# One engine for a whole step: who spreads the turned pages in the compression of a decoder's paged cache

## What is computed

```python
def compress_rows(a, pe, w1, w2):
    n = a.shape[0] // CMP_STRIDE
    seg = a.reshape(n, CMP_STRIDE, N_KV, HEAD_DIM)
    nxt = jnp.concatenate([seg[1:], jnp.zeros_like(seg[:1])], axis=0)
    blk = jnp.concatenate([seg, nxt], axis=1) + pe[None, :, None, :]
    flat = blk.transpose(0, 2, 1, 3).reshape(n, N_KV, CMP_LEN * HEAD_DIM)
    return jax.nn.gelu(flat @ w1) @ w2
...
    k_cmp = compress_rows(rows[:, 0], pe[0], w_c1[0], w_c2[0])
    v_cmp = compress_rows(rows[:, 1], pe[1], w_c1[1], w_c2[1])
```

## Time and profile before

| | us |
|---|---|
| median of 3 runs | 2296.28 (2295.02 to 2296.4) |
| the profiled execution | 2291.58 |
| its span in the profile | 2289.8 |
| the compression stage in it | 971.15 to 1216.00 |
| PE busy in the span | 2010.6 (88%) |
| VectorE busy | 1374.4 (60%) |
| ScalarE busy | 927.0 (40%) |

### The profile page before, as it was taken

The page is one execution under the profiler, slowest core; times in us unless marked ns, Lnnn a source line. Parts: engine busy times, 40 slices in busy tenths (PEclk is TensorE's granted clock), DMA queues, the critical chain, the costliest instruction groups (busy, mean ns, idle before and its releaser), DMA issues.

```text
span 2289.8 us, 28365 instructions
## 1 busy us (share of the span) xinstructions
PE 2010.6 (88%) x10404; PEld 1589.5 (69%) x10404; DVE 1374.4 (60%) x1788; ACT 927.0 (40%) x1229; POOL 115.7 (5%) x154
## 2 busy tenths in 40 slices
PE   5997767879999986599996878799999999999994
PEld 3655523669997454577774556688888888888883
DVE  4423685337773123377774222588888888888885
ACT  0112001100000011167762441277777777777773
POOL 0000000000001000000000000011001111111000
PEclk8997555689999976599997887799999999999997
DMA  7433003044566320034434873289999999999993
GB/s 274 147 101 80 1 6 115 1 129 154 168 176 220 129 102 0 8 122 137 148 120 139 297 293 107 88 322 358 364 351 343 346 342 346 346 354 355 369 346 116
DMA packets 194637, 453.18 MB, mean 198 GB/s; under 512 B 11719, under 2 KB 77375, under 8 KB 193250
## 3 DMA queue, kind: packets, MB, share of 16 engines
q1 hardware_dynamic: 187082, 414.64, 51.5%
q0 software_dynamic: 7456, 37.24, 5.0%
HBM read 439.04 MB, written 21.27 MB: 201 GB/s over the span
## 4 chain that ended last, share of the span: by engine, by line
PE 70%; DVE 8%; ACT 3%; issue 3%; DMA 2%; SPq 1%; POOLq 0%; DVEq 0%; POOL 0%; ACTq 0%
PE bank L2196 63%; PE bank L2199 7%; ACT arena L2692 2%; SPq L2062 1%; DMA arena<-in_cache_nsa 1%; ACT L2692 1%; DVE uT L2455 0%; DMA ring<-in_cache_nsa 0%; DMA arena<-in_w_moe_gu 0%; ACT ring L2692 0%; DVE arena L2590 0%; DMA ring<-scr_y,mkv 0%; DVE arena L794 0%; DVE rtmp L2448 0%; ACT arena_r L2692 0%
## 5 line engine op out<-in xcount | busy, mean ns | idle before, releaser
L2196 PE MATMUL bank<-arena_r 128*128 128x448 f32 (+2 forms) x3296 | 812.9, 361 | 18.3 <-DVE uT_r L648 11.3
L2196 PEld LDWEIGHTS bank<-arena_r 128*128 128x128 f32 x3296 | 607.0, 189 | 94.7 <-issue 15.4
L1680 DVE TENSOR_TENSOR ring_r<-ring,arena_r 128x1792 fp32r<-128x1792 f32 (+1 forms) x216 | 443.8, 2088 | 49.0 <-ACT arena_r L2692 47.6
L2692 ACT ACTIVATE arena_r<-ring 128x1792 fp32r<-128x1792 f32 (+1 forms) x216 | 370.2, 1727 | 136.0 <-PE bank L2196 133.2
L2196 PE MATMUL bank<-arena 128*32 128x256 f32 (+20 forms) x1498 | 284.2, 386 | 60.6 <-DVE arena L2576 25.0
L2692 ACT ACTIVATE arena<-bank 128x512 f32<-128x512 f32 (+11 forms) x312 | 138.6, 457 | 369.5 <-PE bank L2196 243.1
L2196 PEld LDWEIGHTS bank<-arena 128*128 128x128 f32 (+13 forms) x1498 | 194.9, 202 | 131.6 <-issue 69.2
L2196 PE MATMUL bank<-ring_r,arena_r 128*128 128x448 f32 (+1 forms) x840 | 246.0, 374 | 0.0
L2692 ACT ACT_TABLE_LOAD x57 | 73.1, 1283 | 425.3 <-DVE rtmp L2448 144.7
L2199 PE MATMUL bank<-consts_sb,arena 128*128 128x128 f32 (+9 forms) x788 | 143.7, 318 | 106.8 <-DVE arena L794 19.5
L2199 PEld LDWEIGHTS bank<-consts_sb,arena 128*128 128x128 f32 (+9 forms) x788 | 97.4, 160 | 162.6 <-issue 43.2
(11 more groups left out here) (341 smaller groups left out, 1904.2 us busy)
## 6 DMA issues: line engine op xcount, KB each, us to landing
ring<-in_w_moe_gu SPq DMA_DIRECT2D x144, 896.0 KB, 7.0
ring<-in_w_moe_d SPq DMA_DIRECT2D x60, 1024.0 KB, 6.6
ring<-in_cache_nsa SPq DMA_DIRECT2D x176, 256.0 KB, 4.5
arena<-in_w_moe_gu SPq DMA_DIRECT2D x48, 896.0 KB, 6.3
ring<-in_w_ffn_gu SPq DMA_DIRECT2D x22, 1024.0 KB, 7.4
arena<-in_cache_nsa SPq DMA_DIRECT2D x80, 256.0 KB, 6.1
ring<-in_w_in_a SPq DMA_DIRECT2D x8, 1536.0 KB, 7.8
arena<-in_w_moe_d SPq DMA_DIRECT2D x12, 1024.0 KB, 6.7
```

The costliest lines, as they stand in the source:

```text
L1680: V.tensor_tensor(unit_low(c), unit_slot(c), unit_high(c), ALU.subtract).then_inc(S("m_sp"), 1)
L2196: return nc.tensor.matmul(out, lhsT, rhs, start=first, stop=last, **kw_)
L2692: return nc.scalar.activation(out, in_, fn, **kw_)
```

## The change

ScalarE makes all four copies of the even steps and VectorE all four of the odd steps. PE's waits follow: a turn waits for one engine only, the one that copied the bank two steps before, and a group's product for two steps of each. VectorE's and ScalarE's other work keeps its steps; on a step that an engine doesn't copy it also no longer waits for the turn.

```diff
@@ turn(t), on PE
-                for part in range(2):
-                    pe.wait_ge(S(f"xe{part}"), 4 + t - 1)
+                if t == 0:
+                    pe.wait_ge(S("xe0"), 4)
+                    pe.wait_ge(S("xe1"), 4)
+                if t >= 2:
+                    pe.wait_ge(S(f"xe{t % 2}"), 4 + t // 2)
@@ mul(t), on PE
                 if t % 4 == 0:
                     for part in range(2):
-                        pe.wait_ge(S(f"xe{part}"), 4 + t + 4)
+                        pe.wait_ge(S(f"xe{part}"), 4 + t // 2 + 2)
@@ compress_dve
             for t in range(STEPS):
-                dve.wait_ge(S("ct"), 4 + t + 1)
-                if t % 4 == 0:
-                    dve.wait_ge(S("cm"), 2 + max(0, t - 8))
-                for r in range(2):
-                    link(V.tensor_copy(*piece(t, 1, r)), "xe1", r == 1)
+                if t % 2:
+                    dve.wait_ge(S("ct"), 4 + t + 1)
+                    if t % 4 == 1:
+                        dve.wait_ge(S("cm"), 2 + max(0, t - 9))
+                    for n in range(4):
+                        link(V.tensor_copy(*piece(t, n // 2, n % 2)), "xe1", n == 3)
@@ compress_act
             for t in range(STEPS):
-                act.wait_ge(S("ct"), 4 + t + 1)
-                if t % 4 == 0:
-                    act.wait_ge(S("cm"), 2 + max(0, t - 8))
-                for r in range(2):
-                    link(f(*piece(t, 0, r), ACT.Copy), "xe0", r == 1)
+                if t % 2 == 0:
+                    act.wait_ge(S("ct"), 4 + t + 1)
+                    if t % 4 == 0:
+                        act.wait_ge(S("cm"), 2 + max(0, t - 8))
+                    for n in range(4):
+                        link(f(*piece(t, n // 2, n % 2), ACT.Copy), "xe0", n == 3)
```

## The result

| | before | changed |
|---|---|---|
| median, us | 2292.60 (13 runs, 2287.91 to 2296.40) | 2305.50 (13 runs, 2297.69 to 2309.75) |
| profiled execution, us | 2291.58 | 2308.17 |
| span of the profile, us | 2289.8 | 2306.4 |
| first turn (step 0) to last turn (step 127), us | 243.13 | 255.58 |

The changed kernel takes 1.0056 times as long, 95% interval 1.0046 to 1.0066: 12.9 us slower. The median of before is 2292.60 over the 13 runs, where the three shown earlier gave 2296.28.

A forecast was written before the change was run, and what follows sets the result against it. The prediction took PE to bound the 244.85 us stage; A +1.3, B +0.5, C +1.3, D +0.9 and E +2.7 summed to +6.7 us, moving the median from 2296.28 to 2303.0, range 2297 to 2309.

The forecast's parts named there:

- C: VectorE's prompt outputs, which PE's scores await: +3.3 us in six odd steps, -2.0 in five even steps, together +1.3.
- E: ScalarE's gelu and table loads, once per sample: longer copies around them make PE wait longer, +2.7 us.
- B: Odd steps after a wide VectorE score: steps 21 and 101 lose 0.24 each, +0.5 us; step 71 already stalls.
- D: The first 13 steps, with VectorE's query spreading and PE's clock still rising: +0.9 us.
- A: Seven bare odd steps: four VectorE copies need 2.68 us between turns 2.50 apart, stalling PE 0.18 each, +1.3 us.
- Rival 1: Delays absorbed: E is nil as ScalarE reaches its gelu chain earlier; +4.0 us, 2300.3 or 2299.8; within 0.2%, chance 0.33.
- Rival 3: More is lost: late VectorE items delay the next, C, B and E cost more; +14.3 us, 2310.6; chance 0.1.
- rival 2: Free steps win: ScalarE's prompt work and gelu move into its free odd steps; -5.2 us, 2291.1; chance 0.07.
- held rule: VectorE's four copies alternate partition halves, so each waits for the last to finish; sum stays +6.7 us, overlapping leaves +4.9.

The follow-up runs named there:

- e1: Changed kernel with VectorE's prompt output made ahead of its four copies in odd steps; median 2302.02 us, ratio to before 1.0039.
- e6: Kernel before with two extra 256-column ScalarE copies ahead of each gelu in samples 1 to 7; ratio to before 1.0046.
- e10: Changed kernel, outputs ahead of copies in odd steps, gelu in step 7 for samples 1, 2, 3, 6, 7; 2290.86 us, ratio to before 0.9997.
- e8: Changed kernel without the prompt's work; first to last turn 191.55 us, against 190.28 for the kernel before without it.
- e4: Changed kernel with engines swapped: VectorE copies the even steps, ScalarE the odd ones; ratio to before 1.0021.
- e9: Kernel before with outputs ahead of copies in every step, gelu in step 7 for samples 1, 3, 6; 2289.18 us, ratio to before 0.9992.
- e2: Changed kernel with each sample's gelu moved from step 8 to step 7; ratio to before 1.0022.
- e3: Changed kernel with outputs ahead of copies in odd steps and gelu in step 7; ratio to before 1.0018.
- e5: Kernel before with gelu in step 7 and VectorE's prompt output ahead of its copies in every step; ratio to before 0.9996.

## Why the forecast was right in sign and half in size

**Right.** The sign and its chance (slower 0.60), the range (2297 to 2309 holds 2305.5), and for what it named the mechanism: few places, not all steps. C to 0.1 us in the odd steps, PE's resume behind the output in step 17 to 0.01 (3.33 for 3.32); e1 took it away. E to 0.5. B's two steps. The size was not: +12.9 lies above the +4.6 to +11 that had 0.50.

**Wrong, by step of the working.**
- *The clock was held at full rate.* The sum took each wait at its own length. PE's longer waits after gelu were followed by half clock in samples 2, 6 and 7, +4.8 us; e6 made the same thing in the old kernel. The fault was in "E, gelu": I costed the waits and not the half clock that may follow them. That is the larger part of the missing 5.7 us in the stage.
- *D, +0.9 for 2.15.* By step 6 the forecast held (0.8 forecast, 0.85 measured). Then the clock rose near 984.5 instead of 980.7; step 8 alone lost 0.93. How much the start loses is not fixed: e10, whose first 12 steps are the changed kernel's own, stands at +3.0 at step 14, with the clock up 14.8 us after the first turn and not 13.0, and e6 lost 0.7 in before's own steps. So some of D may be where the clock happened to rise.
- *A, +1.3 for 0.* The distance of two weight loads was taken for PE's deadline; e8 shows it for all odd steps.
- *B, step 71.* I wrote that it has such a stall already. I missed that VectorE's sum of step 70 (line 1355, 0.68) now stands between the wide score and the copies. PE's turn of step 73 waits for the copies (1.02 in the weight loads' row):

```profile
1112.54 0.69 DVE L1550 TENSOR_REDUCE small<-arena 128x2 f32<-128x512 f32 x1
1113.26 0.68 DVE L1358 TENSOR_TENSOR arena<-bank,arena 64x508 f32<-64x508 f32 x1
...
1113.98 1.73 DVE L1378 COPY arena<-bank 64x256 f32<-64x256 f32 x4
...
1115.76 0.20 PEld L2204 LDWEIGHTS bank<-consts_sb,ring 128*128 128x128 f32 x2 [1.02 <-DVE arena L1378]
```

- *The base.* The median of before came out 3.7 lower than the three runs shown, which hid part of the missing size in the absolute time. That the range held was in part luck: from the shown 2296.28, the measured +12.9 gives 2309.2, just outside it.
- *Rival 1* put E at nil; it was 3.2. *Rival 3* named losses in all of C, B and E; they did not come, though the total of 12.9 came near its 14.3. In *rival 2* the listed stalls add up to 5.4 and not 5.5, on which nothing hangs.

What the copies cost with banks apart: 1.73 for four on VectorE, where I took 1.75. The pieces that VectorE always made (o = 1) take 0.427 as before, so reading another bank than ScalarE is worth nothing; the pieces that it took over (o = 0) take 0.417 (hence a mean of 0.422). With the held rule of the Trainium skill that the forecast quotes, the trace agrees: no copy overlaps the one before it, each starts 0.013 after that one's end (0.417 + 0.417 + 0.427 + 0.428 + 3 x 0.013 = 1.73).

**The clock in rows.** The sharpest case for E and the clock together is sample 6 of the changed kernel. PE waits 1.62 for a ScalarE copy that stands behind copies, table load and gelu, and 0.8 later it is at half rate: the four product instructions at 1183.71 take 1.91, where they take 1.03 at 1179.08.

```profile
1178.29 1.28 ACT L2697 ACT_TABLE_LOAD   x1
...
1179.08 1.03 PE L2201 MATMUL bank<-uT,arena 128*128 128x256 f32 x4
1179.58 1.47 ACT L2697 ACTIVATE arena<-arena 64x508 f32<-64x508 f32 x2
1181.08 2.18 ACT L2697 ACTIVATE arena<-bank 128x512 f32<-128x512 f32 x5
...
1181.73 1.33 PE L2201 MATMUL bank<-arena 128*128 128x64 f32 x8 [1.62 <-ACT arena L2697]
...
1183.71 1.91 PE L2201 MATMUL bank<-uT,arena 128*128 128x256 f32 x4
```

The same wait, 1.62 at 1020.10 in sample 1, was followed by no dip. And e1, whose sample 2 waits as the changed kernel's does, kept the full clock there. Over the traces of all twelve kernels PE waits twelve times for 1.4 us or more in this stage after its start, and five of them were followed by half clock within 2 us of their end; the other five dips stand behind waits of 0.92 to 0.97, four of them with another of 0.6 to 1.0 shortly before. e4 has seven waits of 1.1 to 1.5 and no dip. So a wait of this size makes half clock possible and does not force it; what decides between such cases stays open. The Trainium skill ("TensorE: Matmul & The Clock Gate", Part 1: The HAM clock gate) says that hardware sets TensorE's clock to one of two rates by how busy it has been. The traces agree: 1.00 and 0.50 are the only levels, and each dip in the stage after its start stands next to a wait of PE of 0.9 us or more.

## What to carry to other kernels

Giving one engine whole steps halves the number of waits and doubles the latency of each step, which cost nothing in the bare steps here, where the consumer comes two steps later; look instead for what else stands in that engine's queue in the steps that it now owns, and whether the consumer waits for it. Move that work to the engine's free steps, one place at a time, and look at what is in the new step first (sample 4 lost 3.8 us to a move that helped five others). When TensorE bounds a stage, allow for more than the length of its waits of about a microsecond and above: some were followed by a stretch at 1.2 GHz that cost 1.5 us or more, most were not. And compare two layouts only after fitting the other work to each: e10's stage is 0.5 us longer than before's and 4.3 longer than e9's.

## What the runs showed of the hardware

- Waits of PE of 0.92 to 1.73 us, most of them behind gelu, were followed in 8 places of five traces (three in the changed kernel, two in e1, one each in e2, e3 and e5) by 3.4 or 6.8 us at a granted clock of 0.50, and e6 added two behind waits of 1.56 and 1.75. Three of the stretches cost 1.5 to 1.7 us each in the changed kernel, measured against the same steps of before; the double one in e6 cost 3.3. Other waits up to 1.75 us were followed by none.
- A turn can start 0.05 us after VectorE's last copy (1008.56 to 1008.61). In before, where a turn waits for two semaphores, it was about 0.115 after VectorE's last copy and 0.05 after ScalarE's; why they differ is not shown.
- VectorE's copies of 64 partitions x 256 elements take 0.417 us for o = 0 (the lower half of the bank's partitions) and 0.427 for o = 1 (line 1378 in the changed kernel, means over 64 steps; r makes no difference). o also sets the columns that are written, and no run tells the two apart. The next copy starts 0.013 after the end of the last where nothing is waited for, and 0.034 after it where the engine waits for its own semaphore (before).
